# Key and value projections of the MoBA heads as one 2x2 block product in seven block products, with the key transposes last

## What is computed

```python
h = rmsnorm(x, mix_norm_g[l])
u = h @ w_in[l]
ml_qk, ml_v, ml_o, ml_i, ml_f, mb_q, mb_k, mb_v = jnp.split(u, splits, axis=-1)
...
q_b = rmsnorm(heads(mb_q, Hb), q_norm_g[l]) * scale
k_b = rmsnorm(heads(mb_k, Hb), k_norm_g[l])
v_b = heads(mb_v, Hb)
h_b = moba_attention(q_b, k_b, v_b)
...
x = x + concatenate([h_m, h_b]) @ w_out[l]
x = x + moe_ffn(rmsnorm(x), ...)      # 32 experts, top 4
x = x + sigmoid(rmsnorm(x) @ w_ple_gate[l]) * (p[l] @ w_ple_proj[l])
```

## Time and profile before

| | us |
|---|---|
| Median of 3 runs | 1095.73 (1095.69 to 1096.56) |
| The profiled execution, own time | 1097.34 |
| Its span | 1095.5 |
| PE busy in it | 1063.8 |
| DVE, ACT, POOL busy | 284.6, 146.9, 45.6 |
| Moved by DMA | 431.88 MB, mean 394 GB/s |

### The profile page before, as it was taken

The page is one execution under the profiler, slowest core; times in us unless marked ns, Lnnn a source line. Parts: engine busy times, 40 slices in busy tenths (PEclk is TensorE's granted clock), DMA queues, the critical chain, the costliest instruction groups (busy, mean ns, idle before and its releaser), DMA issues.

```text
span 1095.5 us, 11997 instructions
## 1 busy us (share of the span) xinstructions
PE 1063.8 (97%) x5118; PEld 445.2 (41%) x5118; DVE 284.6 (26%) x547; ACT 146.9 (13%) x291; POOL 45.6 (4%) x59
## 2 busy tenths in 40 slices
PE   9999999999999999999998999898989899999998
PEld 5485563434343434343433333333333243534335
DVE  4286441232121212121211111121112011211126
ACT  4134350100000000000000000000000110000014
POOL 2422400000000000000000000000000000000000
PEclk9999999999999999999999999999999999999999
DMA  9942779999999999999999999999999999999991
GB/s 348 364 176 105 305 327 425 427 407 430 427 427 435 429 431 430 433 429 429 434 429 434 429 430 430 433 433 430 427 434 427 432 431 430 433 429 424 423 372 42
DMA packets 33788, 431.88 MB, mean 394 GB/s; under 512 B 5207, under 2 KB 5727, under 8 KB 16582
## 3 DMA queue, kind: packets, MB, share of 16 engines
q1 hardware_dynamic: 33520, 431.06, 93.4%
q10 hardware_dynamic: 214, 0.04, 0.0%
HBM read 430.04 MB, written 1.06 MB: 394 GB/s over the span
## 4 chain that ended last, share of the span: by engine, by line
PE 69%; DMA 29%; DVE 1%; issue 0%; ACT 0%; DVEq 0%; ACTq 0%
PE hu L1258 25%; DMA ring<-in_w_gate_up 23%; PE po L1288 15%; DMA ring<-in_w_down 6%; PE aux L1201 6%; PE hu L1053 3%; PE aux L1209 3%; PE hu L844 3%; PE hu L1250 2%; PE hu L850 2%; PE hu L887 1%; PE aux L1465 1%; PE hu L1080 1%; PE hu L860 1%; PE po L1265 1%; PE aux L1234 1%
## 5 line engine op out<-in xcount | busy, mean ns | idle before, releaser
L1258 PE MATMUL hu<-ring,num_xg 128*64 128x512 f32 x1920 | 435.3, 600 | 18.0 <-DMA ring<-in_w_gate_up 17.6
L1258 PEld LDWEIGHTS hu<-ring,num_xg 128*64 128x64 f32 x1920 | 131.9, 137 | 301.7 <-issue 271.3
L1288 PE MATMUL po<-ring,arena 128*64 128x512 f32 x976 | 217.5, 597 | 6.7 <-DMA ring<-in_w_down 6.7
L1880 DVE TENSOR_SCALAR arena<-hu 128x512 f32<-128x512 f32 x31 | 21.4, 692 | 427.8 <-PE hu L1258 427.8
L1288 PEld LDWEIGHTS po<-ring,arena 128*64 128x64 f32 x976 | 70.0, 138 | 149.3 <-issue 145.6
L1856 DVE TENSOR_TENSOR arena<-arena,aux 128x512 f32<-128x512 f32 x58 | 37.3, 684 | 133.1 <-PE aux L1209 121.3
L1201 PEld LDWEIGHTS aux<-num_xg,big 128*128 128x128 f32 x512 | 58.4, 192 | 13.0 <-issue 13.0
L1201 PE MATMUL aux<-num_xg,big 128*128 128x128 f32 x512 | 61.4, 278 | 0.0
L1869 DVE TENSOR_SCALAR arena<-iota_s,posm,gates 128x128 f32<-128x128 f32 x64 | 17.8, 342 | 118.3 <-PE po L1288 115.3
L2240 ACT ACTIVATE hu<-arena 128x512 f32<-128x512 f32 x31 | 18.6, 602 | 196.4 <-DVE arena L1880 196.4
L2256 ACT COPY arena<-po 128x512 f32<-128x512 f32 x16 | 9.4, 586 | 221.8 <-PE po L1278 221.8
(11 more groups left out here) (315 smaller groups left out, 707.6 us busy)
## 6 DMA issues: line engine op xcount, KB each, us to landing
ring<-in_w_gate_up SPq DMA_DIRECT2D x44, 4096.0 KB, 36.4
ring<-in_w_down SPq DMA_DIRECT2D x22, 4096.0 KB, 36.0
ring<-in_w_gate_up SPq DMA_DIRECT2D x37, 2048.0 KB, 15.1
ring<-in_w_down SPq DMA_DIRECT2D x14, 2048.0 KB, 16.5
ring<-in_w_in SPq DMA_DIRECT2D x6, 2048.0 KB, 16.2
ring<-in_w_down SPq DMA_DIRECT2D x8, 1024.0 KB, 33.2
ring<-in_w_gate_up SPq DMA_DIRECT2D x6, 1024.0 KB, 7.8
ring<-in_w_out SPq DMA_DIRECT2D x2, 2048.0 KB, 11.9
```

Of the source, the lines that this page charges most:

```text
L1258: last = mm(hu[n * SLOTS:(n + 1) * SLOTS, 2 * e + b, :], rows_of[:, k, e * SLOTS:(e + 1) * SLOTS], features(w[:, o:o + D], n), start=first ...
L1288: last = mm(bank[n * SLOTS:(n + 1) * SLOTS, :], actT[:, f, h * SLOTS:(h + 1) * SLOTS], w[:, o:o + NB], start=(h == 0 and f == 0), stop=(h ...
L1880: v.tensor_scalar(glu, hu[:, 2 * e, :], LIMIT, None, ALU.min).then_inc(glu_ready, 1)
```

## The change

The key and value sections (chunks 1 and 2) are no longer four jobs of eight matmuls, but one block product of the token blocks (tile by half of K) with the weight blocks (half of K by section) in seven products of four matmuls. `lead_p` (`hu[0]`), `lead_q` and `lead_r` (`po[0]`, `po[1]`) are the PSUM banks. The first two products are plain (tile 0 with the value weights), the others take the sums s1 to s4 and the differences n1 to n4. n1 (in `num_xg`), n2 (in `big1`), n3 (in the key slot itself) and n4 (over n2) are 128x2048 and are made by DVE. ACT makes three copies of partial sums (to `vb[0]`, `lead_m5`, `lead_u2`). The values of tile 0 are the first sum plus `lead_q`, the keys of tile 1 are `lead_p` plus `lead_m5`, those of tile 0 `lead_r` plus `lead_u2`, and both key halves are summed by DVE into `normed`, in SBUF, squared and normalized from there; `normed` has four parts now. The values of tile 1 are what is last in `lead_p`.

The counts of the later block product shift by the three copies (`LEAD_COPIES`). POOL makes s1 and s2 ahead of its wait for the gates, t1 waits for the fourth new product also and t2 for the seventh. SP issues the second half of `w_out` after `negbc`. Line numbers of the changed kernel are larger: `product` is L940, `norm_transposes` L953, the first scores L999, the normalization of keys L1576.

The diff, cut to its core:

```diff
+        n1 = num_xg[:, 0:4 * NB].rearrange("p (k n) -> p k n", n=NB)
+        n2 = big1[:].rearrange("p (k n) -> p k n", n=NB)
+        n3, n4 = kb_weights(0), n2
+        lead_u2, lead_m5 = big2[:, 0:NB], big2[:, NB:2 * NB]
+        lead_p, lead_q, lead_r = hu[:, 0, :], po[:, 0, :], po[:, 1, :]
...
             pe.wait_ge(xs_ready, TT)
-            job(2)
+            pe.wait_ge(normed_ready, 1)
+            wait_chunk(pe, 1)
+            wait_chunk(pe, 2)
+            product(lead_p, token_block(0, 0), vb_weights(0), True, False).then_inc(lead_ps, 1)
+            product(lead_q, token_block(0, 1), vb_weights(1), True, True).then_inc(lead_ps, 1)
+            pe.wait_ge(row_sums, 2)
+            pe.wait_ge(lead_step, 1)
+            product(lead_r, s1, n1, True, False).then_inc(lead_ps, 1)
+            pe.wait_ge(lead_step, 2)
+            pe.wait_ge(part_copied, 1)
+            product(lead_p, s2, n2, False, False).then_inc(lead_ps, 1)
             norm_transposes(0)
...
-            job(3)
+            pe.wait_ge(row_sums, 3)
+            pe.wait_ge(lead_step, 3)
+            pe.wait_ge(part_copied, 3)
+            product(lead_p, s3, n3, False, False).then_inc(lead_ps, 1)
             norm_transposes(1)
-            job(4)
+            pe.wait_ge(row_sums, 4)
+            product(lead_r, s4, kb_weights(1), False, True).then_inc(chunk_done, 1)
+            pe.wait_ge(lead_step, 5)
+            product(lead_p, token_block(1, 1), n4, False, True).then_inc(chunk_done, 1)
             norm_transposes(2)
             norm_transposes(3)
-            job(5)
...
                 if i < TT:
+                    q = hu[:, i, :].rearrange("p (h d) -> p h d", h=H)
                     v.scalar_tensor_tensor(out=out, in0=q, scalar=stat[:, 16 + i:17 + i], in1=inv, op0=ALU.mult, op1=ALU.mult)\
                      .then_inc(normed_ready, 1)
                 else:
-                    v.tensor_tensor(out, q, inv, ALU.mult).then_inc(normed_ready, 1)
+                    v.tensor_tensor(out, out, inv, ALU.mult).then_inc(normed_ready, 1)
...
+            wait_chunk(dve, 1)
+            wait_chunk(dve, 2)
+            v.tensor_tensor(n1, kb_weights(0), vb_weights(0), ALU.subtract).then_inc(lead_step, 1)
             dve.wait_ge(gate_act, 2)
...
+            dve.wait_ge(chunk_done, 1)
+            dve.wait_ge(lead_step, 1)
+            v.tensor_tensor(n2, kb_weights(1), n1, ALU.subtract).then_inc(lead_step, 1)
+            normed_half(1)
+            dve.wait_ge(part_copied, 1)
+            dve.wait_ge(lead_ps, 2)
+            v.tensor_tensor(vb[:, 0, :], vb[:, 0, :], lead_q, ALU.add).then_inc(vb_ready, 1)
+            v.tensor_tensor(n3, kb_weights(1), kb_weights(0), ALU.subtract).then_inc(lead_step, 1)
+            normed_transposed(0)
...
+            v.tensor_tensor(n4, vb_weights(1), n2, ALU.subtract).then_inc(lead_step, 1)
+            dve.wait_ge(lead_ps, 5)
+            dve.wait_ge(part_copied, 2)
+            v.tensor_tensor(normed[:, 2, :], lead_p, lead_m5, ALU.add).then_inc(lead_step, 1)
+            normed_transposed(1)
+            normed_half(2)
+            dve.wait_ge(chunk_done, 2)
+            dve.wait_ge(part_copied, 3)
+            v.tensor_tensor(normed[:, 3, :], lead_r, lead_u2, ALU.add).then_inc(lead_step, 1)
+            normed_half(3)
+            normed_transposed(2)
             normed_transposed(3)
...
+            block_squares(1)
+            act.wait_ge(lead_ps, 1)
+            a.copy(vb[:, 0, :], lead_p).then_inc(part_copied, 1)
+            block_roots(1)
+            act.wait_ge(lead_ps, 3)
+            a.copy(lead_m5, lead_r).then_inc(part_copied, 1)
+            act.wait_ge(lead_ps, 4)
+            a.copy(lead_u2, lead_p).then_inc(part_copied, 1)
...
+            act.wait_ge(chunk_done, 3)
+            a.copy(vb[:, 1, :], lead_p).then_inc(vb_ready, 1)
```

More of the change, by code:

```diff
@@ L305, in hybrid_layer @@
         og_ready = sem("og_ready")
+        lead_ps = sem("lead_ps")
+        lead_step = sem("lead_step")
         row_sums = sem("row_sums")
@@ L415, in hybrid_layer, with kb_weights, vb_weights @@
         t3 = o_weights(0)
+        LEAD_COPIES = 3
+        def kb_weights(half):
+            return slot(1, NB, K)[:, 4 * half:4 * half + 4, :]
+        def vb_weights(half):
+            return slot(2, NB, K)[:, 4 * half:4 * half + 4, :]
+        n1 = num_xg[:, 0:4 * NB].rearrange("p (k n) -> p k n", n=NB)
[3 more added lines that the diff above has]
+        lead_p, lead_q, lead_r = hu[:, 0, :], po[:, 0, :], po[:, 1, :]
         def wo_weights(half, n):
@@ L483, in wait_job @@
             else:
-                eng.wait_ge(job_ps, sum(not last_of_chunk(i) for i in range(j + 1)))
+                eng.wait_ge(job_ps, sum(not last_of_chunk(i) for i in range(j + 1) if i < 2 or i >= J_QK))
         def selections(pair):
@@ L575, in _ @@
                          .to_broadcast([P, H * S])).then_inc(negbc_loaded, 16)
+            load(CHUNK_WO_B, slot(CHUNK_WO_B, D, 4), w_out_k[:, 4:8, :])
             load(CHUNK_WO_A, slot(CHUNK_WO_A, D, 4), w_out_k[:, 0:4, :])
@@ L839, in job @@
                     wait_chunk(pe, n)
[L840 to L851, removed]
+                ct = (j - J_QK) % 4
+                for k in range(K):
+                    last = mm(bank[:, 0:S], slot(n, NB, K)[:, k, ct * P:(ct + 1) * P], hT[:, k, :],
+                              start=(k == 0), stop=(k == K - 1))
                 done_job(j, last)
@@ L926, in _, with product @@
             done_job(1, raw_job(1, range(2, K)))
+            def product(bank, rows_of, weights, first, last):
+                for k in range(4):
+                    ins = mm(bank, rows_of[:, k, :], weights[:, k, :], start=(first and k == 0), stop=(last and k == 3),
+                             skip_group_check=True)
+                return ins
             def norm_transposes(i):
@@ L1047, in output_transposes @@
                 last.then_inc(hmT_ps, 1)
[L1050 to L1055, removed]
             sum_p, sum_q, sum_r = hu[:, 0, :], hu[:, 1, :], hu[:, 2, :]
@@ L1775, in _ @@
             dve.wait_ge(chunk_done, 6)
[L1776 removed]
+            dve.wait_ge(part_copied, LEAD_COPIES + 1)
             v0 = vx[:, 0, :, 0:DH]
@@ L2054, in _, with block_squares @@
             act.wait_ge(root_warm, 1)
-            for i in range(4):
-                wait_job(act, J_NORM + i)
-                if i >= 2:
-                    act.wait_ge(nstat, 2 * (i - 2) + 1)
+            def block_squares(i):
                 sq = sq_junk[:, i % 2 * W:(i % 2 + 1) * W]
                 if i < TT:
+                    wait_job(act, J_NORM + i)
                     act.wait_ge(rstd_ready, i + 1)
-                    a.activation(sq, hu[:, i % 2, :], ACT.Square, scale=stat[:, 16 + i:17 + i]).then_inc(sq_ready, 1)
+                    a.activation(sq, hu[:, i, :], ACT.Square, scale=stat[:, 16 + i:17 + i]).then_inc(sq_ready, 1)
@@ new lines, in _ @@
+            block_roots(0)
+            act.wait_ge(gate_step, 3)
+            a.activation(fln, fneg, ACT.Exp).then_inc(gate_act, 1)
+            act.wait_ge(gate_act, 1)
+            a.activation(fln, fln, ACT.Ln, bias=1.0).then_inc(gate_act, 1)
+            block_squares(1)
[4 more added lines that the diff above has]
+            a.copy(lead_m5, lead_r).then_inc(part_copied, 1)
@@ L2076, in _ @@
+            act.wait_ge(lead_ps, 4)
+            a.copy(lead_u2, lead_p).then_inc(part_copied, 1)
             act.wait_ge(gcol_ps, 1)
             act.dma_start(negm_d, negm).then_inc(negm_stored, 16)
+            for i in range(2, 4):
+                block_squares(i)
+                block_roots(i)
             a.activation(emc[:].rearrange("p t h -> p (t h)"), hu[:, 3, 0:TT * H], ACT.Exp).then_inc(emc_ready, 1)
-            for tt in range(TT):
-                wait_job(act, J_VB + tt)
-                a.copy(vb[:, tt, :], hu[:, tt, :]).then_inc(vb_ready, 1)
+            act.wait_ge(chunk_done, 3)
```

60 lines of the change are left out of this document (26 added, 34 removed).

## The result

The changed kernel takes 1099.35 us (median of 11 runs, 1097.97 to 1100.85) against 1096.58 us (11 runs, 1095.46 to 1096.87) for the kernel before on the same chip. The ratio is 1.0028, with a 95% interval of 1.0021 to 1.0036: about 3 us lost. The forecast was 1096.9 us and no change that can be measured, in a range up to 1098.0. It was counted from the median of the first three runs of the kernel before, 1095.73 us, so 0.85 us of the distance to 1099.35 is that median and no mechanism: forecast was +1.2 us, measured +2.8.

What follows compares the result with a forecast made beforehand. PE's progress until about 150 us, then the expert stream's bytes, bound the kernel. The products' 3.4 us goes into PE's waits; with a clock fall +1.2 us on the 1095.73 median gives 1096.9 us, range 1094.8 to 1098.0.

Steps and rivals of the forecast that it cites:

- the seven products without a wait of PE: Key and value sections on PE: seven products take 24.0 us, 3.4 us less, with no wait worth counting, ending at 49.6.
- DVE's second normalization held by POOL: Last key half: DVE's instruction with two SBUF inputs waits for POOL's first difference, ending at 52.3 us; scores at 53.9.
- a fall of the clock: PE's clock falls to 1.2 GHz after nearly 4 us with 0.45 us of work; 6 in 10, costs 1.7 us.
- the wait of L1659 for POOL's third difference: DVE's pair before the conv steps waits until POOL's third difference ends at 61.4 us; PE's job at 64.4, +0.6 us.
- the carry of what PE has at 64 us to the end: A shift of PE's third conv job, at 63.84 us before, reaches the kernel's end whole.
- Rival 3: DVE's normalization gets through only behind POOL's second difference; job at 68.0 us, +4.2 us, 1099.9 us; chance 0.10.
- Rival 1: DVE's instruction with two SBUF inputs does not wait for POOL; PE at 63.9 us, +0.1 us, 1095.8 us; chance 0.16.
- Rival 2: POOL's differences come earlier, PE is bound by itself; job at 61.2 us, -2.6 us, 1093.1 us; chance 0.10.
- that the change does not touch: POOL's first weight difference, started by a DMA landing, still runs from 47.19 to 51.70 us.
- What is moved without effect: SP's later second w_out half, POOL's earlier s1 and s2 and ACT's value copy change no time.
- with a fall 11.2: Start of scores to third conv job takes 11.2 us instead of 9.5 at a fallen clock; job at 65.1 us.
- The handover term: DVE's 0.69 us instruction gets between POOL's first and second differences, pushing the later ones by 0.6 us, to 61.4.

Runs made afterwards that it cites:

- e1: Changed kernel with the last key half's sum kept in its PSUM bank, so the normalizing instruction has one SBUF input; 1098.59 us, ratio 1.0023 to the kernel before.
- e4: Changed kernel with POOL's first two weight differences held until heads 0 and 1 are normalized, the third until heads 2 and 3; 1093.95 us, ratio 0.9976.
- e2: Changed kernel with the second w_out half issued ahead of the router, bias and negbc loads again; 1097.75 us, ratio 1.0013 to the kernel before.
- e7b: Kernel before the change, with PE's first scores also waiting for POOL's second weight difference; 1099.60 us, ratio 1.0034.
- e5b: Kernel before the change, with POOL's weight differences held until heads 0 and 1, then 2 and 3, are normalized; 1095.88 us, ratio 0.9995.
- e3: Changed kernel with 26 dummy transposes before the last key transposes and 8 behind them, while PE waits; 1098.12 us, ratio 1.0019 to the kernel before.

## Why the prediction was wrong, step by step

Right, with their numbers: the seven products without a wait of PE, to 49.64 us (49.6); the two transposes behind them exposed; DVE's second normalization held by POOL, and for the reason given, the second SBUF input (e1); a fall of the clock (6 in 10); the wait of L1659 for POOL's third difference; the gain of 3.4 us gone into PE's waits; the carry of what PE has at 64 us to the end. Rival 3 did not come: L1576 got through between POOL's first and second difference. Rival 1 fell with e1 and e4. Rival 2, "POOL is out of the way", is e4: -2.43 us at the job, where I had worked out -2.6.

What failed are two terms: one put at nothing, one too small. The sum had 65.1 us for the job and it was 67.09.

1. The step that POOL's first difference is started by the landing of a DMA "that the change does not touch", and with it "What is moved without effect". The change moves the load behind it, and the landing came 0.91 us later (48.10 against 47.19). All of POOL's work, DVE's wait and the scores moved with it: 54.72 us against 53.9 worked out, 0.8 us. I had counted the moved loads as without effect, since I looked only for who reads them, and not for what they share the DMA engines with. e2 shows the term: with the old order of loads POOL starts at 47.22 us again and the job comes 0.97 us earlier, though PE's clock falls there too.
2. The step "with a fall 11.2". The row that I took it from cost 1.7 us, after a single wait of 2.63 us, though I had said in the same place that PE would stand longer here than in either row; e7b gives 1.6 us for a single wait in this very place. In the changed kernel there are two, 2.98 and 0.84 us, with four transposes between, and the clock stayed at 0.50 for over 6 us: scores and conv jobs took 65.49 - 54.72 = 10.77 us instead of 7.87, so 2.9 us (e2, with waits of 2.17 and 0.84 us: 2.6). From the scores to the job it was 12.37 us and not 11.2. I had named a range of +0.9 to +1.5 us around one value, where the cost is the half speed of whatever work lies in the slow stretch, and the stretch was not bounded by the row.

The two give 0.8 and 1.2 us, together the 2.0 us from 65.1 to 67.09. The handover term was too large, but off the path: DVE's instruction pushed POOL's second difference by 0.33 us (4.84 us instead of 4.51), not by 0.6.

The chances were wrong in consequence. That slower by over 0.2% needed rival 3 was itself a mistake: both unknown costs lay on the same side, and 1.0 us more on top of the +1.2 us with a fall makes 2.2 us.

What stays open: how much of the shift the expert stage gives back. Near the end (SP's last weight loads, issued at 1043.79 us before and 1045.29 after) the profiled pair differs by 1.5 us, and the medians differ by 2.8. Single profiles scatter by 1 to 2 us there (e5b's issue of the last weights is 2.2 us before that of the kernel before, with a job only 0.58 us earlier), and I did not separate it.

## What to carry to other kernels

Before giving DVE an instruction with a second input in SBUF, look at what POOL runs at that moment: here two waits that hold POOL's work back to a time in which nobody waits for DVE were worth 5.7 us at the job, against the 1.9 us of the products. Keeping the one sum in PSUM gave only 1.5 us, since the next DVE instruction then ran into POOL. A saving on the engine that binds is only collected if the next in line is early as well, so follow the chain to the first job that nothing else delays, and ask what else is tied to a fixed event, here the landing of a DMA. And a wait of PE such as those here (2.56 us, or 2.98 and 0.84) can cost more than half as much again behind it by its clock: price it by the work that will follow at half speed, and fill it if it can't be removed.

## What the runs showed of the hardware that I had not expected

A load queued behind another can delay the first one's landing: with the router, bias and negbc loads behind it, POOL was released by the last 2 MB section at 48.10, 48.61 and 48.80 us (changed kernel, e3, e1); with the next 2 MB section behind it at 47.19 and 47.29 us (before, e7b), and with nothing at 47.22 us (e2). From 45 to 47 us in the changed kernel the DMA engines were counted fully busy (1.19) at 228 GB/s.

DVE got in between two POOL instructions that stand back to back, but for one instruction only; this was seen in one place. In e1 the first of the two TENSOR_SCALAR of L1659 came through as POOL's second difference ended, and the second, directly behind it, then took 4.61 us, until the third difference ended. These TENSOR_SCALAR have one tile as input, in SBUF, and one number for each partition, and with POOL idle the pair takes 0.55 us; so a second tile in SBUF is not needed for being held, and what is needed was not tested.

With POOL's instruction started first, a DVE TENSOR_TENSOR with one PSUM input and one SBUF input was not slowed at all (0.69 us beside a running POOL difference), and the one with two SBUF inputs was held for the whole (4.08 and 4.85 us). The start of e1's is only 0.05 us behind POOL's, but the bias addition, which reads one tile in PSUM and one in SBUF, shows it too: in the changed kernel it ran well inside POOL's second difference (52.69 to 57.53 us), in e4 beside an idle POOL.

```profile
56.49 0.55 DVE L1645 SCALAR_TENSOR_TENSOR arena<-ring,po 128x384 f32<-128x384 f32 x1 [1.83 <-PE po L999]
...
52.98 0.56 DVE L1647 SCALAR_TENSOR_TENSOR arena<-ring,po 128x384 f32<-128x384 f32 x1 [1.11 <-PE po L1001]
```

The Trainium skill, page "SBUF — State Buffer", section "Who interferes with whom", has this distinction, and both halves of it are confirmed here by the same instruction with the one operand changed.
